# One encoder layer on one core: the order of the token mixers is rewritten

## What is computed

```python
h = layer_norm(concat(meta, x))
proj = h @ w_in                       # 2048 x 13376: c_q 512, c_kv 512, k_r 64, rq, rk, rv, rg, ga, gb 2048 each
q = rms_norm(c_q) @ w_uq              # 16 heads x (128 + 64 rotary)
kv = rms_norm(c_kv) @ w_ukv           # 16 heads x (128 key + 128 value); k_r, rotated, is shared by all heads
o_a = softmax(mask(q @ k.T * scale)) @ v        # per head; a row sees its own chunk of 64 and earlier ones
o_b = silu(rg) * group_norm(retention(rq, rk, rv))   # 8 heads x 256, in chunks of 64
merged = sigmoid(ga) * (o_a @ w_pa) + sigmoid(gb) * (o_b @ w_pb)
h = layer_norm(ALPHA * h + merged @ w_out)
h = layer_norm(ALPHA * h + moe(h))    # top-1 of 4 groups, top-2 of 8 experts in it, SwiGLU 2048-512-2048
```

## Time and profile before

| | us | share of the span |
|---|---|---|
| profiled execution | 2395.54 | |
| span | 2393.7 | |
| PE busy, 11545 matmuls | 2203.8 | 92% |
| DVE busy | 1577.6 | 66% |
| ACT busy | 1243.1 | 52% |
| mean granted clock of PE | 0.933 | |
| data read from HBM | 590.9 MB | 255 GB/s with 18.87 MB written |

### The profile page before, as it was taken

The page is one execution under the profiler, slowest core; times in us unless marked ns, Lnnn a source line. Parts: engine busy times, 40 slices in busy tenths (PEclk is TensorE's granted clock), DMA queues, the critical chain, the costliest instruction groups (busy, mean ns, idle before and its releaser), DMA issues.

```text
span 2393.7 us, 30553 instructions
## 1 busy us (share of the span) xinstructions
PE 2203.8 (92%) x11545; PEld 1825.2 (76%) x11545; DVE 1577.6 (66%) x1338; ACT 1243.1 (52%) x1007; POOL 96.2 (4%) x74
## 2 busy tenths in 40 slices
PE   4798889999999999899897899999999999999991
PEld 3776667888999999688786777777777777777771
DVE  5433332443545455544535799999999999999996
ACT  2322223443333232233422588888888888888870
POOL 1000000000000000000100000000000000000000
PEclk9977777999999999899998799999999999999995
DMA  4411213565544444355644299999999999999983
GB/s 157 145 62 62 66 54 103 189 204 164 185 159 159 157 159 146 100 192 193 213 141 181 110 416 411 406 421 412 420 412 419 408 419 409 416 405 421 410 347 143
DMA packets 153498, 598.04 MB, mean 250 GB/s; under 512 B 15648, under 2 KB 19856, under 8 KB 102080
## 3 DMA queue, kind: packets, MB, share of 16 engines
q1 hardware_dynamic: 149760, 589.60, 64.8%
q0 software_dynamic: 3680, 7.64, 1.0%
HBM read 590.90 MB, written 18.87 MB: 255 GB/s over the span
## 4 chain that ended last, share of the span: by engine, by line
PE 72%; DVE 14%; issue 9%; ACT 2%; DMA 1%; POOL 0%; DVEq 0%; SPq 0%; ACTq 0%; POOLq 0%
PE ps L1488 19%; PE ps L1474 13%; PE ps L864 9%; DVE wl L618 8%; PE ps L865 8%; PE ps L861 5%; PE ps L845 3%; PE ps L886 2%; PE ps L1536 2%; PE ps L1557 1%; PE ps L1580 1%; PE ps L1578 1%; ACT wh L507 1%; PE ps L1548 1%; DVE yall L743 1%
## 5 line engine op out<-in xcount | busy, mean ns | idle before, releaser
L618 DVE TENSOR_TENSOR wl<-raw,wh 128x2048 fp32r<-128x2048 f32 x352 | 786.8, 2287 | 58.7 <-ACT wh L507 57.5
L507 ACT ACTIVATE wh<-raw 128x2048 fp32r<-128x2048 f32 x352 | 665.0, 1913 | 122.6 <-PE ps L865 73.4
L1168 DVE TENSOR_TENSOR wl<-raw,wh 128x2048 fp32r<-128x2048 f32 x161 | 368.9, 2292 | 498.2 <-ACT wh L1028 498.2
L1028 ACT ACTIVATE wh<-raw 128x2048 fp32r<-128x2048 f32 x161 | 308.1, 1914 | 631.9 <-PE ps L1488 301.2
L864 PE MATMUL ps<-wh,xg 128*128 128x512 f32 x900 | 383.5, 426 | 0.9 <-issue 0.7
L865 PE MATMUL ps<-wl,xg 128*128 128x512 f32 x900 | 360.6, 401 | 0.0
L1474 PE MATMUL ps<-hth,wh 128*128 128x272 f32 (+1 forms) x896 | 261.2, 291 | 15.4 <-DVE wl L1168 9.9
L1474 PE MATMUL ps<-htl,wh 128*128 128x272 f32 (+1 forms) x896 | 258.6, 289 | 0.0
L1474 PE MATMUL ps<-hth,wl 128*128 128x272 f32 (+1 forms) x896 | 258.2, 288 | 0.0
L864 PEld LDWEIGHTS ps<-wh,xg 128*128 128x128 f32 x900 | 173.9, 193 | 52.6 <-DVE wl L618 9.7
L864 PE MATMUL ps<-wh,hx 128*128 128x512 f32 x508 | 204.9, 403 | 3.4 <-DVE hx L736 3.4
(11 more groups left out here) (320 smaller groups left out, 3227.3 us busy)
## 6 DMA issues: line engine op xcount, KB each, us to landing
raw<-in_w_dram SPq DMA_DIRECT2D x384, 1024.0 KB, 8.2
raw<-in_w_in_dram SPq DMA_DIRECT2D x104, 1024.0 KB, 5.1
raw<-in_w_pa_dram SPq DMA_DIRECT2D x16, 1024.0 KB, 5.0
raw<-in_w_pb_dram SPq DMA_DIRECT2D x16, 1024.0 KB, 5.0
raw<-in_w_out_dram SPq DMA_DIRECT2D x16, 1024.0 KB, 5.1
raw<-in_w_ukv_dram SPq DMA_DIRECT2D x8, 1024.0 KB, 5.3
raw<-in_w_uq_dram SPq DMA_DIRECT2D x8, 768.0 KB, 4.5
yrow<-yscr SPq DMA_DIRECT2D x4, 1024.0 KB, 10.8
```

What stands on the lines that cost most here:

```text
L507: nc.scalar.activation(wh2[:, x % HELD, :], raw2[:, slot2(x), :], ACT.Copy).then_inc(s_wh2, 1)
L618: nc.vector.tensor_tensor(wl2[:, slot2(x), :], raw2[:, slot2(x), :], wh2[:, x % HELD, :].bitcast(F32), ALU.subtract).then_inc(s_wl2, 1)
L1028: nc.scalar.activation(wh[:, n % 2, :], raw1[:, n % RING1, :], ACT.Copy).then_inc(s_wh, 1)
L1168: nc.vector.tensor_tensor(wl[:, n % 2, :], raw1[:, n % RING1, :], wh[:, n % 2, :].bitcast(F32), ALU.subtract).then_inc(s_wl, 1)
```

## The change

- The ring: `wl` now lies where `raw1` lies (`lo` writes over the landed weights), and `wh` and `wl` have four slots. The load of unit n waits for `s_wused` of unit n-4; so do, for the first round, loads 4 to 7 of the experts. `hi` and `lo` run three units ahead of PE in the lists instead of two.
- The start: x is loaded in two tiles, each with a semaphore, and `moments`, a root and `normalise` run per tile; `lo(0)` stands between the last tile's moments and its normalising. ACT applies scale and offset (`affine`, four buffers), DVE makes `hth` and `htl`. PE transposes 8 blocks, then weaves 4 each behind the first two units of c_kv, which come first now.
- The latents: c_kv's squares are summed behind the first unit of c_q, c_q's behind the rotary key's unit. The further steps of each (`mean_square`, `root`, `scale_latents`, `latent_hi`, `latent_lo`) stand in the lists of DVE and ACT between the `hi` and `lo` of later units.
- The heads: first eight units of w_ukv, all keys and values kept in SBUF (`kn`, `vx`, `vm`), then eight units of w_uq, all queries kept (`qn`, `qro`). The w_uq load is split in three so that it lands in the order that the products use. PSUM banks alternate between units.
- Attention: 16 gate units (the columns ga), and behind gate unit i PE does `weigh(i-2)`, `turn_probs(i-1)` and `attend(i)` of single heads; the last two stand behind the first two units of w_pa. The sigmoid goes to `mrg` itself, and `merge_a` multiplies the product with w_pa into it. The mask product takes fp32r operands (`rowmask_r`, `ones_r`) in place of float32.
- Retention, the second gates, w_out and the experts keep their order on PE; in the lists of ACT and DVE their `hi` and `lo` stand one unit further ahead.

```diff
-N_C = 0
-N_MLA = N_C + 9
-N_GA = N_MLA + 2 * MLA_PAIRS
-N_RET = N_GA + 32
+N_CKV = 0
+N_CQ = N_CKV + 4
+N_KR = N_CQ + 4
+N_KV = N_KR + 1
+N_Q = N_KV + MLA_PAIRS
+N_GA = N_Q + MLA_PAIRS
+N_PA = N_GA + 16
+N_RET = N_PA + 16
...
-        wh = place("wh", [P, 2, U], 65536, F32R)
-        wl = place("wl", [P, 2, U], 81920, F32R)
+        wl = place("wl", [P, RING1, U], 0, F32R)
+        wh = place("wh", [P, RING1, U], 65536, F32R)
+        kn = place("kn", [P, H_MLA, LT], A0)
+        qn = place("qn", [P, H_MLA, SEQ], 133120)
+        vx = place("vx", [P, TT, H_MLA * VH], 183296)
...
-                        sp.wait_ge(s_wl, N_UNITS)
+                        sp.wait_ge(s_wused, N_UNITS)
...
-                need(sp, s_wl, n - RING1 + 1 + 4 * turn if n >= RING1 or not isinstance(turn, int) or turn else 0)
+                need(sp, s_wused, n - RING1 + 1 + 4 * turn if n >= RING1 or not isinstance(turn, int) or turn else 0)
...
+            sp.dma_start(xme[:, :], ins["meta"]).then_inc(s_x[TT], 16)
+            for t in range(TT):
+                sp.dma_start(xin[:, t, :], ins["x"][0, P * t:P * (t + 1), :]).then_inc(s_x[t], 16)
...
+            for g in range(MLA_PAIRS):
+                load(N_KV + g, 0, unit_view(raw1, (N_KV + g) % RING1), rows(w_ukv, 0, 512 * g))
+            for g in range(MLA_PAIRS):
+                n = N_Q + g
+                sp.wait_ge(s_wused, n - RING1 + 1)
+                dst = unit_view(raw1, n % RING1, 384)
+                src = rows(w_uq, 0, 384 * g, 384)
+                head = NOPE + ROPE
+                for to, at, width in ((0, 0, head), (head + ROPE, head, NOPE), (head, head + NOPE, ROPE)):
+                    sp.dma_start(dst[:, :, to:to + width], src[:, :, at:at + width]).then_inc(s_raw[n % RING1], 16)
...
+            def affine(b):
+
+                act.wait_ge(s_tr, b + 1)
+                need(act, s_hl, b - 3)
+                nc.scalar.activation(ht_tmp[:, b % 4, :], ps[:, b % 4, 0:LT], ACT.Identity, bias=lnb[:, b:b + 1],
+                                     scale=lng[:, b:b + 1]).then_inc(s_hv, 1)
...
+            def latents(j, last):
+                act.wait_ge(s_wused, last + 1)
+                b = LAT_BANK[j]
+                nc.scalar.activation(clat[:, j, :, :], ps[:, b:b + 4, 0:LT], ACT.Copy)
+                nc.scalar.activation(csq[:, j, :, :], ps[:, b:b + 4, 0:LT], ACT.Square).then_inc(s_lat, 1)
+            def key_copy(g):
+                act.wait_ge(s_wused, N_KV + g + 1)
+                b = 4 * (g % 2)
+                nc.scalar.activation(kn[:, 2 * g:2 * g + 2, :], ps[:, b:b + 2, 0:LT], ACT.Copy).then_inc(s_kc, 1)
+            def query_copy(g):
+                act.wait_ge(s_wused, N_Q + g + 1)
+                b = 2 * (g % 4)
+                nc.scalar.activation(qro[:, 2 * g + 1, :], ps[:, b + 1, 0:SEQ], ACT.Copy).then_inc(s_qc, 1)
+                nc.scalar.activation(qn[:, 2 * g:2 * g + 2, :], ps[:, b, :].rearrange("p (a q) -> p a q", a=2),
+                                     ACT.Copy).then_inc(s_qc, 1)
...
+            def mean_square(j, count):
+                dve.wait_ge(s_ss, count)
+                nc.vector.tensor_scalar(crs[:, j, :], ps[:, SS_BANK[j], 0:LT], 1.0 / RANK, EPS, ALU.mult,
+                                        ALU.add).then_inc(s_sv, 1)
+            def value_copy(g):
+                dve.wait_ge(s_wused, N_KV + g + 1)
+                b, c = 4 * (g % 2), 2 * VH * g
+                nc.vector.tensor_copy(vx[:, :, c:c + 2 * VH], ps[:, b + 2, :].rearrange("p (t c) -> p t c", t=TT))
+                nc.vector.tensor_copy(vm[:, c:c + 2 * VH], ps[0:N_META, b + 3, 0:2 * VH]).then_inc(s_vc, 1)
...
+            hi(0)
+            act.wait_ge(s_const, 16 * N_CONST)
             for b in range(KD):
+                affine(b)
+                if b in (7, 11):
+                    hi(b // 4)
+            nc.scalar.activation(rowmask_r[:, :], rowmask[:, :], ACT.Copy)
+            nc.scalar.activation(ones_r[0:1, 0:64], ones[0:1, 0:64], ACT.Copy).then_inc(s_msk, 1)
             nc.scalar.activation(alh[:, :], alf[:, :], ACT.Copy).then_inc(s_alh, 1)
+            hi(3)
+            for n in range(1, N_GA):
+                if n == N_KV:
+                    act.wait_ge(s_wused, N_KR + 1)
+                    nc.scalar.activation(krt[:, :], ps[:, 4, 0:LT], ACT.Copy).then_inc(s_krc, 1)
+                hi(n + 3)
+                if n == N_CQ:
+                    latents(1, N_CQ - 1)
+                if n == N_CQ + 1:
+                    root(1, 1)
+                if n == N_CQ + 2:
+                    latent_hi(1, 1)
+                if n == N_KR:
+                    latents(0, N_KR - 1)
+                if N_KV < n <= N_Q:
+                    key_copy(n - N_KV - 1)
+                if n == N_KV + 1:
+                    root(0, 2)
+                if n == N_KV + 2:
+                    latent_hi(0, 2)
+                if n > N_Q:
+                    query_copy(n - N_Q - 1)
+            for i in range(H_MLA + 2):
+                hi(N_GA + i + 3)
+                if i == 0:
+                    query_copy(MLA_PAIRS - 1)
+                if i >= 2:
+                    transposed(i - 2)
+                if 1 <= i <= H_MLA:
+                    softmax(i - 1)
+                if i >= 4 and i % 4 == 0:
+                    sigmoid_a(i // 4 - 1)
...
+            moments(*tiles[0])
+            moments(*tiles[1])
+            normalise(0, *tiles[0])
+            normalise(1, *tiles[1])
+            moments(*tiles[2])
+            lo(0)
+            normalise(2, *tiles[2])
+            for b in range(KD):
+                dve.wait_ge(s_hv, b + 1)
+                nc.vector.tensor_scalar_mul(hth[:, b, :], ht_tmp[:, b % 4, :], 1.0).then_inc(s_hh, 1)
                 dve.wait_ge(s_hh, b + 1)
+                nc.vector.tensor_tensor(htl[:, b, :], ht_tmp[:, b % 4, :], hth[:, b, :].bitcast(F32),
                                         ALU.subtract).then_inc(s_hl, 1)
+                if b in (7, 11):
+                    lo(b // 4)
...
+            for n in range(1, N_GA):
+                lo(n + 3)
+                if n == N_CQ + 1:
+                    mean_square(1, 1)
+                if n == N_CQ + 2:
+                    scale_latents(1, 1)
+                if n == N_CQ + 3:
+                    latent_lo(1, 1)
+                if n == N_KV + 1:
+                    mean_square(0, 2)
+                    rotary_key()
+                if n == N_KV + 2:
+                    scale_latents(0, 2)
+                if n == N_KV + 3:
+                    latent_lo(0, 2)
+                if N_KV < n <= N_Q:
+                    value_copy(n - N_KV - 1)
+                if n >= N_Q + 2:
+                    rotary_queries(n - N_Q - 2)
+            for i in range(H_MLA + 3):
+                if i >= 3:
+                    store_head(i - 3)
+                if i < H_MLA + 2:
+                    lo(N_GA + i + 3)
+                if i < 2:
+                    rotary_queries(MLA_PAIRS - 2 + i)
+                if 1 <= i <= H_MLA:
+                    maxima(i - 1)
+                    probabilities(i - 1)
+            for n in range(N_PA + 2, N_RET):
+                lo(n + 3)
+                if n > N_PA + 4 and (n - N_PA) % 4 == 0:
+                    merge_a((n - N_PA) // 4 - 1)
+                if n == N_PA + 4:
+                    merge_a(0)
+            merge_a(3)
...
+            for b in range(8):
+                turn_input(b)
             for u in range(4):
+                pe.wait_ge(s_hl, 4 * u + 4)
+                t_unit(N_CKV + u, 0, u, [(4 + b, 0, True) for b in range(4)])
+                if u < 2:
+                    for b in range(4 * u + 8, 4 * u + 12):
+                        turn_input(b)
             for u in range(4):
+                t_unit(N_CQ + u, 0, u, [(b, 0, True) for b in range(4)])
+                if u == 0:
+                    square_sums(1, 1)
...
+            def keys(g):
+
+                n = N_KV + g
+                pe.wait_ge(s_wl, n + 1)
+                need(pe, s_kc, g - 1)
+                if g == 1:
+                    pe.wait_ge(s_sv, 2)
...
+            def attend(h):
+
+                g, a = divmod(h, 2)
                 pe.wait_ge(s_qc, 2 * g + 2)
+                pe.wait_ge(s_qr, g + 1 if h > 1 else MLA_PAIRS - 1)
+                need(pe, s_ptc, h - 1)
...
+                    m = nc.tensor.matmul(ps[:, 4 + h % 2, c0 + kt - 64:c0 + kt], rowmask_r[:, :], ones_r[0:1, 0:64],
...
+            pe.wait_ge(s_cl, 1)
+            for g in range(MLA_PAIRS):
+                keys(g)
+                values(g)
             pe.wait_ge(s_cl, 2)
+            for g in range(MLA_PAIRS):
+                queries(g)
+                if g:
+                    rotate(g - 1)
+            for i in range(H_MLA + 2):
+                if i < H_MLA:
+                    c, u = divmod(i, 4)
+                    if u == 0 and c < 2:
+                        pe.wait_ge(s_qr, 5 + c)
+                    elif u == 0:
```

(88 more changed lines are left out.)

566 lines of the change are left out of this document (204 added, 362 removed).

## The result

The changed kernel took 2333.61 us (median of 4 runs, 2330.24 to 2334.25); its ratio to the kernel before is 0.9744, 95% interval 0.972 to 0.9769. The forecast was 2330 us, between 2308 and 2368.

The account below looks back on a forecast made before the run. Of the MLA pairs' 246 us the low clock was taken as the largest loss. Retention was to start at 488 instead of 564.1, gain 76, less 10 for clock falls: 66 us faster, 2330 us, range 2308 to 2348 (stated range 2308 to 2368).

Parts of the forecast that it names:

- Start: Front of the kernel: PE starts about 19.8 us, first dense unit about 26 against 46.35, four units end at 55.7.
- my pace per block: Transposes of x at the start: 0.8 us of PE time for each of 16 blocks.
- The queue behind `hi` and `lo`: Ahead of retention: copies PE needs queue behind conversions awaiting loads; 3.3 us before each sum, 10.0 before key unit 1.
- my 7.9: Later key units: 7.9 us per unit, since key_copy(g) is done 7.2 + 0.6 after unit g.
- The steps: Attention between gate units: 10.2 us of work, 10.4 by the chain of waits, so 0.2 us stall per step.
- The clock carried by dense work: Attention steps: each head's attention lies between two dense units, so it was taken at the full clock level.
- the slower rival: Attention stays at the lower clock in all 16 steps, 7.2 us per step: 39 us slower, 2436; chance 0.06.
- the one of every second step: Clock falls in every second attention step: eight steps cost 39 us, gain 37, 2360 us; chance 0.17.
- Late landing: Ring loads land in 8.2 us, not 5.1: 65 us lost, nothing gained, 2395; chance 0.07.
- My sentence that the row shows no such loss: w_uq load: rope key loads in 256 B rows landed in 5.2 us, so no short-row loss; otherwise 4 us more.
- the falls: Where a stall or non-dense stretch lowers the clock, a unit loses 2.6 us; four falls counted, +10 us.
- Four of my own signs: Among the signs of being right: masks under 0.2 us, step clock over 0.9, retention starting at 485 to 505, no longer.

Follow-up runs that it names:

- the kernel without waits: Changed kernel with every small operation PE waits for, up to the last attention step, put ahead of `hi` or `lo`: 2268.16 us, 0.9487 to the kernel before.
- the version with attention by itself: Changed kernel with all 16 heads run one behind the other ahead of the 16 gate units: 2382.43 us, 0.995 to the kernel before.
- the second trace of the changed kernel: The changed kernel measured and profiled once more, with no edit: 2335.62 us, 0.9741 to the kernel before.
- the mean square first: Changed kernel with the second mean square and rotary key ahead of the `lo` waiting for key unit 0: 2317.27 us, 0.9685 to the kernel before.
- the copies first: Changed kernel with key, value and query copies and query rotation ahead of the `hi` or `lo` three units further: 2303.05 us, 0.9623 to the kernel before.

## Why the prediction was right

- **Start.** PE starts at 20.2 (19.8 forecast), the first dense unit at 26.5 (26), the fourth unit ends at 56.1 (55.7). The weaving is worth 10.7 us of it, not the 3 that my pace per block gives.
- **The queue behind `hi` and `lo`.** This step carried the working, and it held nearly to the number: 3.3 us before each of the sums (6.3 in two), 10.0 ahead of key unit 1 (10.0). `values(3)` waited 2.9 us where some 2 were forecast, `queries(0)` 1.8 where 2.9 were. Moving the operations ahead of the conversions removed each of these waits. Key units took less than my 7.9: `keys(g)` needs the copy of g-2, so that only each second unit waits. The end of the key units, forecast at 173, came at 176.9, mostly because the first unit started 3.2 us later.
- **The steps.** Forecast 10.4 us, and 0.2 us of stall in it. Two gate units of the whole chain, two steps apart:

```profile
306.93 5.77 PE ps L1539 x24
...
327.95 5.77 PE ps L1539 x24
```

  10.51 us a step at a clock of 1.00, and 10.18 with the stall gone, where the least was put at 10.2. The masks take 0.22 us each, not 0.1.
- **The clock carried by dense work.** Attention alone stays at 0.50 even at full occupancy, and between gate units at 1.00: that rules out the slower rival and the one of every second step for this kernel. Late landing is out too: loads of w_in land in 5.1 us, and the last part of w_uq 5.4 us after a slot is free (5.5 forecast). The part in rows of 256 B, 128 KB, lands in 3.7 us, the larger ones in 3.4 and 4.0. So the Trainium skill's loss for rows under 512 B (DMA: Bandwidth & Descriptors, Specifications) costs the sum nothing. It is there all the same: in this trace a packet of 256 bytes takes 19.2 ns on its DMA engine and one of 512 bytes 27.2. My sentence that the row shows no such loss read too much into it, as half a megabyte in short rows took as long there (5.2 us) as a whole one in longer rows (5.1). Of the Trainium skill's two places on the clock (TensorE: Matmul & The Clock Gate), the one on idle gaps, in HAM oscillation, agrees with the kernel without waits, whose clock did not fall once in 373 us. It does not explain 120 us at the lower level without a gap. Nor does the other, in Part 4 of the same page of the Trainium skill, by which transposes do not count: they are 1.1 of the 8.45 us of a head. Which of a head's products leave the clock low stays open.
- **What was mis-sized: the falls.** "I count four such falls: +10" is the step that failed. Ahead of retention there are eleven, 55 us in all at the lower level, a part of it while PE waits; a twelfth begins in the wait for the merge. The query units show it: the trace has, per two units,

```profile
197.71 0.37 SPq L1003
...
199.63 3.47 DMA raw<-in_w_uq_dram
...
203.15 1.36 issue
204.51 0.38 ACT qro L1065
...
204.93 0.70 PE ps L1638 x2
205.63 5.79 PE ps L1630 x36
```

  The "issue" is `hi`. The load chain is as forecast (7.2 us from the end of a unit to the rotation, 7.4 forecast), but after 3 us of waiting the rotation takes 0.70 instead of 0.43 and the next unit 5.79 instead of 4.2. Each of these four falls costs 1.8 us, less than the 2.6 that I took; it is their number that I had wrong. So the pair takes 13.7 us and not 12.05, and gate unit 0 begins at 233.4, not 222.5. The first three steps, with one such wait of 4.5 us, lose 5 more, the rest of them another 5. Retention started 11.4 us after the 498 that the forecast with its falls gives.
- **What was not forecast:** 6.8 us gained from retention on, where I had put 0 with bounds of 4, because only the order of `hi` and `lo` differs there. Of these, 2.5 are the rounds, by the conversions standing one unit further ahead (shown: they go when this is undone). The rest lies at the end of retention and in the second gates, where PE's busy time, not its waits, is shorter at a clock nearer to full. What moved these falls is not shown.

Four of my own signs failed: the masks took 0.22 us where under 0.2 was named, the clock over the first six steps was 0.86 where over 0.9 was, retention started at 509.4 where 505 was the latest, and 6.8 us of the gain sit behind that start.

The two errors have opposite signs, so that 2330 lies nearer to 2333.6 than its terms deserve: 54.7 + 6.8 against 66 + 0.

## What to carry to other kernels

In an in-order engine a conversion that waits for a prefetch holds up every small operation behind it; where PE waits for that operation, put it ahead of the conversion, and where PE waits for the conversion, leave it behind. Here one reordering of lists, with no instruction changed, was worth as much as the whole rewrite. Count for each wait of PE what the clock takes after it as well as the wait, and place work that does not raise the clock between work that does.

## What was not expected of the hardware

- In the version with attention by itself, PE is busy for 120 of 120 us with float32 products of one head at a time, and stays at a granted clock of 0.50. In the version with all small operations first, 4.7 us of the same work between two gate units run at 1.00 in all of the 161 us from 200 to 361.
- After each wait of 2 to 3 us in the query units a part of the next unit ran at the lower level; with the waits gone the clock did not fall there. Shorter waits can come ahead of a fall too: the one at 411 to 417 us in the second trace of the changed kernel began 2 us after a wait of 0.8 us. The traces of three other versions (the mean square first, the copies first, the start without weaving) have such falls late in the steps too, each 1 to 2 us after a wait of 0.5 to 1.0 us. Other waits of that length had none after them.
